# Three token mixers of a decoder block: weight splits of the two channel-decay scans placed elsewhere, and the delta scan's row broadcasts done by DMA

## Time and profile before

| what | us |
|---|---|
| median of 3 runs (4169.1 to 4172.25) | 4170.32 |
| the profiled execution, its own time | 4172.02 |
| its span | 4170.3 |
| TensorE busy in the span | 3611.9 (87%) |
| VectorE busy | 2871.7 (69%) |
| ScalarE busy | 831.5 (20%) |
| GpSimd busy | 889.6 (21%) |

### The profile page before, as it was taken

The page is one execution under the profiler, slowest core; times in us unless marked ns, Lnnn a source line. Parts: engine busy times, 40 slices in busy tenths (PEclk is TensorE's granted clock), DMA queues, the critical chain, the costliest instruction groups (busy, mean ns, idle before and its releaser), DMA issues. The chain is left out here.

```text
span 4170.3 us, 40813 instructions
## 1 busy us (share of the span) xinstructions
PE 3611.9 (87%) x14450; PEld 2471.0 (59%) x14450; DVE 2871.7 (69%) x5066; ACT 831.5 (20%) x1654; POOL 889.6 (21%) x844
## 2 busy tenths in 40 slices
PE   5999988778778777777999987986987999999998
PEld 4778875223223222222788866864755787877876
DVE  6653678778878878866664556766867457757775
ACT  1110122111111111101211134314842211411000
POOL 2010004444444434432000011204530000100000
PEclk9999999999999999999999988997998999999999
DMA  6423228999999999996333412128972222232321
GB/s 251 170 81 99 96 101 321 421 423 424 423 423 423 422 420 410 420 417 275 105 115 123 147 66 86 47 80 339 421 278 71 82 96 90 89 101 92 101 86 68
DMA packets 205590, 907.17 MB, mean 218 GB/s; under 512 B 20666, under 2 KB 25546, under 8 KB 126178
## 3 DMA queue, kind: packets, MB, share of 16 engines
q0 software_dynamic: 92368, 662.37, 38.9%
q1 hardware_dynamic: 108128, 233.38, 16.5%
q10 hardware_dynamic: 4900, 8.94, 0.6%
HBM read 875.75 MB, written 40.94 MB: 220 GB/s over the span
## 5 line engine op out<-in xcount | busy, mean ns | idle before, releaser
L130 DVE CAST ring_high<-ring_raw 128x2048 fp32r<-128x2048 f32 (+1 forms) x169 | 198.2, 1173 | 471.1 <-PE psum L178 398.8
L176 PE MATMUL psum<-ring_high,h_features 128*128 128x512 f32 x1128 | 461.7, 409 | 34.9 <-DVE ring_low L132 16.4
L177 PE MATMUL psum<-ring_low,h_features 128*128 128x512 f32 x1128 | 448.9, 398 | 0.0
L178 PE MATMUL psum<-ring_high,h_features 128*128 128x512 f32 x1128 | 448.2, 397 | 0.0
L1630 PE MATMUL psum<-slots_ring,evacuation_tmp 128*128 128x512 f32 x672 | 334.1, 620 | 92.4 <-DVE evacuation_tmp L1724 92.4
L132 DVE TENSOR_TENSOR ring_low<-ring_raw,ring_high 128x2048 fp32r<-128x2048 f32 (+1 forms) x169 | 365.6, 2164 | 13.8 <-issue 1.6
L176 PE MATMUL psum<-h_features,ring_high 128*128 128x512 f32 (+3 forms) x888 | 350.8, 395 | 17.6 <-DVEq L287 9.4
L177 PE MATMUL psum<-h_features,ring_high 128*128 128x512 f32 (+3 forms) x888 | 347.6, 391 | 0.0
L178 PE MATMUL psum<-h_features,ring_low 128*128 128x512 f32 (+3 forms) x888 | 347.1, 391 | 0.0
L1846 ACT ACTIVATE weight<-score 128x1 f32<-128x1 f32 x512 | 103.6, 203 | 1124.9 <-DVE score L1731 1124.7
L1630 PE MATMUL psum<-slots_features,evacuation_tmp 128*128 128x512 f32 x504 | 250.1, 620 | 64.4 <-DVE evacuation_tmp L1724 64.2
(11 more groups left out here) (646 smaller groups left out, 7084.3 us busy)
## 6 DMA issues: line engine op xcount, KB each, us to landing
ring_raw<-in_w_in SPq DMA_DIRECT2D x94, 1024.0 KB, 5.3
ring_raw<-in_w_up_pairs SPq DMA_DIRECT2D x20, 1024.0 KB, 5.0
ada_ring<-in_w_ada POOLq DMA_DIRECT2D x16, 1024.0 KB, 5.6
ring_raw<-in_w_out SPq DMA_DIRECT2D x12, 1024.0 KB, 5.0
moe_entries<-in_const_zero_rows POOLq DMA_DIRECT2D x23, 512.0 KB, 4.2
row_room<-moe_entries SPq DMA_DIRECT2D x23, 512.0 KB, 11.1
moe_results<-rows_out SPq DMA_DIRECT2D x23, 512.0 KB, 7.6
ring_raw<-in_w_down SPq DMA_DIRECT2D x10, 1024.0 KB, 5.0
```

The lines of the kernel that those rows point to most:

```text
L130: nc.vector.tensor_copy(high, whole)
L176: nc.tensor.matmul(out, a[0], b[0], start=start, stop=False)
L177: nc.tensor.matmul(out, a[0], b[1], start=False, stop=False)
L178: return nc.tensor.matmul(out, a[1], b[0], start=False, stop=stop)
```

## The change

1. `close` calls `project` for `gdn_out` with `deferred=bound is not None` instead of `decay is not None`. So in `gdn_out`, and only there, VectorE now also splits half 0 of the gla stage's chunk, before it evacuates `gdn_out`'s second chunk.
2. gla splits its remaining piece (half 1) after VectorE's step 1, which a new `yield` ends after the two differences; its TensorE groups move ahead in the table, and so do the evacuations by the renumbering.
3. hgrn has ScalarE cast both pieces (`cast_piece`, after ScalarE's steps 1 and 2, with another new `yield` after the three first `raise_drop`) and VectorE only subtract (`low_piece`), after its steps 3 and 6, which are one loop step earlier than before. Its TensorE groups are placed anew.
4. In the delta scan the eight unit rows go from `scale_row` to DRAM and back as a broadcast to `squares`, four rows per DMA, all issued by GpSimd; the gate rows go the same way to `row`, which lies over `diag`: two for the first pair of heads after `scanned`, two for the second pair when the levels of the first pair are nearly done. L2074 and L2096 are gone. The inverse blocks of the second pair now wait for `solved` by themselves.

```diff
@@ project_along
             for n, p in enumerate(range(start, 2 * base + 2)):
                 pace.until(side.tables["first"][n] if "first" in side.tables else 0)
-                split_piece(nc, core, dve, p // 2, p % 2)
+                if "cast" in side.tables:
+                    low_piece(nc, core, dve, p // 2, p % 2, cast, n + 1)
+                else:
+                    split_piece(nc, core, dve, p // 2, p % 2)
...
             pace = Pace(side.act, act, sems)
+            if "cast" in side.tables:
+                for n, p in enumerate(range(start, 2 * base + 2)):
+                    pace.until(side.tables["cast"][n])
+                    cast_piece(nc, core, act, p // 2, p % 2).then_inc(cast, 1)
@@ delta_scan, TensorE
-        pe.wait_ge(on.rooted, 1)
-        for f in range(N):
-            if f >= 5:
-                pe.wait_ge(on.unit_scaled, f - 4)
-            nc.tensor.matmul(unit_bank(f), core.ident[0:N, f:f + 1].to_broadcast([N, P]), scale_row[:], start=True, stop=True).then_inc(on.unit_spread, 1)
...
-            nc.tensor.matmul(core.ps[:, 0, :], core.ident[0:H, h:h + 1].to_broadcast([H, P]), g_row[:], start=True, stop=True).then_inc(on.spread, 1)
...
@@ delta_scan, GpSimd
+        pool.wait_ge(on.rooted, 1)
+        pool.dma_start(core.unit_rows, scale_row[:]).then_inc(on.units_kept, 16)
+        pool.wait_ge(on.unit_summed, 1)
+        pool.wait_ge(on.units_kept, 16)
+        for part, spread in enumerate((on.units_spread0, on.units_spread1)):
+            pool.dma_start(squares[:, H * part:H * (part + 1), :], core.unit_rows[H * part:H * (part + 1), :].partition_broadcast(P)).then_inc(spread, 16)
+        pool.wait_ge(on.scanned, 1)
+        pool.dma_start(core.gate_rows, g_row[:]).then_inc(on.rows_kept, 16)
+        pool.wait_ge(on.rows_kept, 16)
+        for h, spread in enumerate((on.spread0, on.spread1)):
+            pool.dma_start(row[:, h, :], core.gate_rows[h, :].partition_broadcast(P)).then_inc(spread, 16)
         for s in range(ROW_TILES):
             pool.wait_ge(on.updated, s + 1)
+            if s == 2 * LEVELS - 2:
+                pool.wait_ge(on.decayed, 2)
+                pool.wait_ge(on.masked, 2 * LEVELS)
+                for h, spread in enumerate((on.spread0, on.spread1)):
+                    pool.dma_start(row[:, h, :], core.gate_rows[2 + h, :].partition_broadcast(P)).then_inc(spread, 16)
@@ delta_scan, VectorE
-            dve.wait_ge(on.unit_spread, f + 1)
-            nc.vector.scalar_tensor_tensor(qkvT[:, f, :], qkvT[:, f, :], GDN_DK ** -0.5 if f < H else 1.0, unit_bank(f), ALU.mult, ALU.mult).then_inc(on.unit_scaled, 1)
+            dve.wait_ge((on.units_spread0, on.units_spread1)[f // H], 16)
+            nc.vector.scalar_tensor_tensor(qkvT[:, f, :], qkvT[:, f, :], GDN_DK ** -0.5 if f < H else 1.0, squares[:, f, :], ALU.mult, ALU.mult).then_inc(on.unit_scaled, 1)
...
+            if half:
+                dve.wait_ge(on.solved, NT)
@@ tables
-GLA_ORDER = {"first": [3, 5], "pe": [1, 3, 5, 7, 9, 11, 13, 15], "dve": [14, 16], "act": [4, 8, 12, 16]}
-HGRN_ORDER = {"first": [3, 6], "pe": [3, 6, 10, 14, 18, 22, 26, 29], "dve": [27, 32], "act": [11, 15, 27, 31]}
+GLA_ORDER = {"first": [1], "pe": [0, 1, 3, 5, 7, 9, 11, 13], "dve": [16], "act": [4, 8, 12, 16]}
+HGRN_ORDER = {"cast": [1, 2], "first": [3, 6], "pe": [4, 6, 9, 12, 16, 20, 24, 28], "dve": [27], "act": [11, 14, 26, 30]}
@@ channel_decay, VectorE
             difference(nc.vector, 1).then_inc(differed, 1)
+            yield
             key_step(0)
@@ close
-                        aside=decay(gate) if decay is not None else None, deferred=decay is not None)
+                        aside=decay(gate) if decay is not None else None, deferred=bound is not None)
```

More of the change, by code:

```diff
@@ L448, in project_along @@
     stashing = any(run[3][0] == "stash" for run in runs)
-    with stage(nc, name, "freed", *[f"stashed{n}" for n in range(NT if stashing else 0)], "evacuated", "loaded", *side.signals) as (block, freed, *sems):
-        stashed, evacuated, sems = sems[0:NT if stashing else 0], sems[NT if stashing else 0], sems[(NT if stashing else 0) + 1:]
+    with stage(nc, name, "freed", *[f"stashed{n}" for n in range(NT if stashing else 0)], "evacuated", "cast", "loaded", *side.signals) as (block, freed, *sems):
+        stashed, evacuated, cast, sems = sems[0:NT if stashing else 0], sems[NT if stashing else 0], sems[(NT if stashing else 0) + 1], sems[(NT if stashing else 0) + 2:]
         @block.sync
@@ L2049, in delta_scan @@
     pick = over(nc, rhs, "pick", [P, N, N])
+    row = over(nc, diag, "spread_row", [P, 2, SEQ])
     kind_beta, kind_cum, kind_minus = 0, 1, 2
@@ L2055, in delta_scan @@
     head = lambda half, n: 2 * half + n
-    unit_bank = lambda f: core.ps[:, 1 + f % 5, :]
-    signals = ("picks", "squared", "unit_summed", "inverted", "rooted", "unit_spread", "unit_scaled", "shifted", "logged", "rated", "scanned",
-               "turned", "valued", "spread", "edged", "decayed", "scored", "applied", "copied_blocks", "masked", "first", "scaled", "second", "updated",
+    signals = ("picks", "squared", "unit_summed", "inverted", "rooted", "units_kept", "units_spread0", "units_spread1", "unit_scaled", "shifted", "logged", "rated", "scanned",
+               "turned", "valued", "rows_kept", "spread0", "spread1", "edged", "decayed", "scored", "applied", "copied_blocks", "masked", "first", "scaled", "second", "updated",
                "gathered", "sided", "solved", "stored", "output", "copied")
@@ L2088, in pe_part @@
         yield
-        def spread_row(half, n):
-            if n == 0:
-                pe.wait_ge(on.valued if half == 0 else on.copied, 1 if half == 0 else 2)
-            else:
-                pe.wait_ge(on.decayed, 2 * half + 1)
-            h = head(half, n)
-            nc.tensor.matmul(core.ps[:, 0, :], core.ident[0:H, h:h + 1].to_broadcast([H, P]), g_row[:], start=True, stop=True).then_inc(on.spread, 1)
         def score(half, n, m):
@@ L2106, in pe_part @@
         for half in range(2):
-            spread_row(half, 0)
+            if half:
+                pe.wait_ge(on.copied, 2)
             yield
+            if half == 0:
+                pe.wait_ge(on.valued, 1)
             score(half, 0, 0)
             yield
-            spread_row(half, 1)
             yield
@@ L2197, in act_part @@
                 act.wait_ge(on.edged, 2 * half + n + 1)
-                decay_strips(nc, core.ps[:, 0, :], edge, lambda s: cols[:, kind_minus, head(half, n), s:s + 1], attn[:, n])
+                decay_strips(nc, row[:, n, :], edge, lambda s: cols[:, kind_minus, head(half, n), s:s + 1], attn[:, n])
                 act.drain().then_inc(on.decayed, 1)
@@ L2253, in make_edge @@
         def make_edge(half, n):
-            dve.wait_ge(on.spread, 2 * half + n + 1)
+            dve.wait_ge((on.spread0, on.spread1)[n], 16 * (half + 1))
             if n or half:
                 dve.wait_ge(on.decayed, 2 * half + n)
-            nc.vector.tensor_tensor(edge[:], core.ps[:, 0, :].rearrange("p (s t) -> p s t", s=NT),
+            nc.vector.tensor_tensor(edge[:], row[:, n, :].rearrange("p (s t) -> p s t", s=NT),
                                     core.causal[:].unsqueeze(1).to_broadcast([P, NT, P]), ALU.add).then_inc(on.edged, 1)
```

4 lines of the change are left out of this document (2 added, 2 removed).

## The result

The changed kernel takes **4127.55 us** (median of 4 runs, 4125.87 to 4130.31) beside 4170.60 (4 runs): a ratio of 0.9899, 95% interval 0.9886 to 0.9911. Its profiled execution took 4125.87, with a span of 4124.1.

What follows compares the result with a forecast made beforehand. TensorE's own work bounds the delta scan, hand-over chains between engines bound gla and hgrn. Terms +0.1 - 20 - 5.7 + 0 - 4.2 = -29.8 us gave 4141 us, own range 4135 to 4147, whole range 4131 to 4157.

Steps and rivals of the forecast that it cites:

- `gdn_out` +0.1: In `gdn_out`, VectorE's added split of 3.5 us fits its idle time of 3.4; last evacuation starts 0.1 us later.
- Gla -20: Gla stage 20 us shorter, bounds -14 and -23: split waits go and slow weight groups run at full clock.
- Hgrn -5.7: Hgrn stage 5.7 us shorter, bounds 0 and -9, from moved weight groups, with ScalarE's casts just hidden.
- Ran slowly behind the first two, for some 1.2 us each: In hgrn, TensorE's low-clock loss behind the first two far-key placement waits, 2.4 us in the sum.
- Part 4 of the prediction: The delta scan's part: head 0 and gate rows -4.2 us, with clock 0.5 behind a wait costing 1.7 and more.
- +2.9, of which 2.0 stay: Hgrn's first weight group, behind score 4, starts 2.9 us later; 2.0 of it remain until the first application.
- 6.45 of waits: In hgrn, TensorE's waits for placements behind VectorE's far keys in three units, 2.46, 2.37 and 1.62 us, removed.
- Rival A: Hgrn gives nothing: the late first group and ScalarE's casts cost what the three waits give; 4147 us, chance 0.15.
- Delta head 0: Delta scan's head gains 0, bounds -10.6 and +13: TensorE's freed 7.25 us turn into two waits, with lost clock.
- Gate rows -4.2: Delta scan's four gate-row matmuls on TensorE, replaced by DMA, are a plain gain of 4.2 us, bounds -4.2 and 0.
- Gla's gates and `gla_out`, 0: The stages between gla and hgrn were forecast to change by 0 us.
- 2 MB in 9.5 us: Delta head: broadcasting the unit rows, 2 MB in two issues, takes 9.5 us; all rows at 2088.5, bounds 2086 and 2102.

Runs made afterwards that it cites:

- hgrn_early: Changed kernel with hgrn's half 0 split in `gla_out`, two weight groups early in hgrn, one cast and one subtraction fewer there: 4138.87 us, 0.9921 to before.
- changed_third: The changed kernel measured once more without any edit, as a third sample: 4127.39 us, 0.9890 to before.
- gla_alone: Kernel before with only the `gdn_out` and gla parts of the change; delta scan and hgrn places as before: 4150.23 us, 0.9956 to before.
- group_at_3: Changed kernel with hgrn's first weight group behind score 3, as before the change, instead of score 4: 4132.82 us, 0.9902 to before.
- units_on_pe: Changed kernel with the 8 unit rows spread by TensorE again, gate rows still by DMA: 4129.21 us, 0.9896 to before.

## Why the prediction was wrong

The mechanisms mostly came as described, the sizes did not: 29.8 us by terms, 37.3 to 39.9 in the stages of the three samples. The term that failed most is hgrn's, 5.7 us forecast and 10.7 measured, because the price of a wait was too low.

- *`gdn_out` +0.1.* Right: 28.4 instead of 28.5, the split stands in VectorE's idle time. `hgrn_early` shows the other side: in `gla_out`, without that cover, it costs its length.
- *Gla -20.* The walk through the queues gave 22, the stage gave 21.9. I took 2 off for a stretch at low clock that did not come in this profile (group clock 1.00); in `changed_third` it did, but cost 0.1 of stage time (clock 0.97, 59.8 us); in `gla_alone` it cost 1.6.
- *Hgrn -5.7.* This is the term that failed. "Ran slowly behind the first two, for some 1.2 us each" was 3.5 and 1.66, 5.2 instead of 2.4: I had counted only a part of the slow stretch, which takes in the scores and far scores between the wait and the weight group as well as the group. Part 4 of the prediction had itself read 1.7 and more for a clock of 0.5 behind such a wait. "+2.9, of which 2.0 stay", charged with the whole 2.9, was 1.4 (`group_at_3`): TensorE gets most of it back in a unit in which it waits for VectorE anyway. With 6.45 of waits, which was right, the terms give 6.45 + 5.2 - 1.4 = 10.2; measured 10.7. Corrected by this term alone, the forecast is 4136, which is still 8 above the measured time and inside the range; the range is missed by what gla, the head, gla's gates and the open remainder add. Rival A was the wrong way round: the casts were hidden, and were worth 1.1.
- *Delta head 0.* Right for three of the eleven profiled executions of this head; in the other eight, the changed kernel's own profile among them, it gave some 1.5. The clock's return behind the second wait decides which. Both waits came, 2.52 and 4.04, and the transposes lost 1.6 at clock 0.50.
- *Gate rows -4.2.* Right: 314.6 to 310.2 with the unit rows still on TensorE, 4.4.
- *Gla's gates and `gla_out`, 0.* They were 0.5 to 1.1 shorter. The waits are the same (7.5 and 1.5 us), TensorE is busy for 47.9 instead of 49.0 us, at 0.92 instead of 0.90: it is clock, and what gave it back is open.
- *The Trainium skill's rule* ("SBUF — State Buffer", section "SBUF: two separate sides"), that a DMA from GpSimd is held while VectorE copies float32: the trace agrees in that the store of the gate rows, issued beside VectorE's cast, took 1.19 us to issue, where that of the unit rows took 0.59 with VectorE idle. `units_on_pe` shows it for the same instruction: there the cast starts 1.9 us later, and the store of the gate rows takes 0.59. The longer issue cost nothing that shows: the rows came later than I said, 49.1 us into the stage (2106.94, forecast up to 2105 for a stage that began 1.4 sooner), but `edge` had been made 51.8 into it before.
- *2 MB in 9.5 us*: 8.1 from the issue to VectorE's use of the second half, 4.8 to the first. The estimate by the Trainium skill, "DMA: Bandwidth & Descriptors", section "Anatomy of one DMA — SWDGE (gpsimd) path", of 6.8 was too low by 1.3.

With the right sizes the forecast would have been 4131 to 4133. The median lies 3 to 6 below that. That remainder is **open**: three comparisons with before show 43.0, 44.6 and 46.6 us, the stages 37.3 to 39.9. The rest of the program was longer in both profiles of before than in all three of the changed kernel, but variants of the changed kernel fill the gap between them, so scatter isn't excluded either.

## What to carry to other kernels

Price a short wait of TensorE by comparing a whole unit of work with and without it, not by the wait and the next group: here one of 2.4 us cost 4 to 6. Independent work belongs where the other engine's longest step is, in every unit: `hgrn_early` took it out of a unit that was full on TensorE to fill one in which TensorE waits for VectorE, and lost in the one without winning in the other. And where a DMA takes the place of matmuls, look at the order of the queue that waits for it; turning that order gave 3 us in the stage, not shown in the kernel's time, the DMA alone none to 1.5.

## What was not expected of the hardware

After the same wait, in the same code, the clock's return differs between executions: the 24 weight matmuls behind the transposes took 5.6 us at 0.99 in one and 6.7 at 0.82 in another, and the delta stage falls into two lengths, 308.2 to 308.9 (eight profiles) and 310.0 to 310.1 (three). Stages that an edit doesn't touch move with the clock too: `gdn_out` 28.3 to 29.9, gla 59.7 and 61.3, hgrn 92.0 and 93.5. A stage's length read from one profile has up to these 1.6 us in it.
